# A two-block transformer forward pass in one kernel: the first norm's root moves to VectorE, and the start of the first feed-forward layer is reordered

## What is computed

```python
def rms_norm(x, w):
    xf = x.astype(jnp.float32)
    y = xf * lax.rsqrt(jnp.mean(xf * xf, axis=-1, keepdims=True) + EPS)
    return (y * w.astype(jnp.float32)).astype(x.dtype)

def modulate(x, w, shift, scale):
    return rms_norm(x, w) * (1 + scale[:, None, :]) + shift[:, None, :]

def swiglu(h, w13, w2):
    gu = jnp.einsum('bsd,df->bsf', h, w13)
    g, u = jnp.split(gu, 2, axis=-1)
    return jnp.einsum('bsf,fd->bsd', jax.nn.silu(g) * u, w2)

    c_act = jax.nn.silu(c)
        mod = (jnp.einsum('bd,dn->bn', c_act, w_ada[l]) + b_ada[l]).reshape(b, N_SUB, 3, D_MODEL)
        h = modulate(x, norm_w[l, 0], mod[:, 0, 0], mod[:, 0, 1])
        x = x + 0.5 * mod[:, 0, 2][:, None, :] * swiglu(h, ffn_w13[l, 0], ffn_w2[l, 0])
```

## Time and profile before

| | |
|---|---|
| median of 3 runs | 1054.44 us (1054.14 to 1054.47) |
| profiled execution | 1055.47 us |
| its span, first to last instruction | 1053.6 us |
| PE busy | 1006.0 us, 95% of the span |
| DVE busy | 753.7 us, 72% |
| ACT busy | 534.7 us, 51% |
| POOL busy | 39.3 us, 4% |
| DMA | 215.10 MB, mean 204 GB/s |

### The profile page before, as it was taken

The page is one execution under the profiler, slowest core; times in us unless marked ns, Lnnn a source line. Parts: engine busy times, 40 slices in busy tenths (PEclk is TensorE's granted clock), DMA queues, the critical chain, the costliest instruction groups (busy, mean ns, idle before and its releaser), DMA issues.

```text
span 1053.6 us, 18959 instructions
## 1 busy us (share of the span) xinstructions
PE 1006.0 (95%) x7848; PEld 971.6 (92%) x7848; DVE 753.7 (72%) x1355; ACT 534.7 (51%) x920; POOL 39.3 (4%) x85
## 2 busy tenths in 40 slices
PE   2999999979798999999999999999999999999996
PEld 1999999979797999999999988799899999999996
DVE  4978998857887687685876488546568865575675
ACT  3644654426366555454565445654446554355443
POOL 2000000034400000000000000000000000000000
PEclk9999999989899999999999999999999999999999
DMA  8877899854383455768764545346554555555411
GB/s 329 320 283 298 314 350 354 295 186 161 134 290 136 156 186 180 269 211 194 261 242 160 173 148 200 123 168 171 139 166 160 206 171 189 185 180 208 155 74 41
DMA packets 34533, 215.10 MB, mean 204 GB/s; under 512 B 3725, under 2 KB 7693, under 8 KB 9614
## 3 DMA queue, kind: packets, MB, share of 16 engines
q1 hardware_dynamic: 34446, 213.88, 58.4%
HBM read 211.25 MB, written 2.62 MB: 203 GB/s over the span
## 4 chain that ended last, share of the span: by engine, by line
PE 81%; DVE 5%; DMA 4%; POOL 4%; ACT 3%; issue 3%; SPq 0%; DVEq 0%; POOLq 0%; ACTq 0%
PE bank L210 79%; DMA sb_raw<-wts 3%; PE bank L213 2%; ACT sb_ring L186 1%; POOL sb_nst L189 1%; DVE sb_tq L189 1%; DMA R<-scratch 1%; ACT sb_tmp L186 1%; DVE sb_ring L189 1%; DMA R<-rows 1%; DVE sb_junk L198 1%; POOL sb_st_a L189 0%; POOL sb_st_v L192 0%; POOL sb_nst L192 0%; DVE R L189 0%
## 5 line engine op out<-in xcount | busy, mean ns | idle before, releaser
L210 PE MATMUL bank<-sb_h,sb_ring 128*128 128x256 f32 (+2 forms) x4224 | 523.3, 284 | 10.3 <-DVE sb_tq L189 7.5
L210 PEld LDWEIGHTS bank<-sb_h,sb_ring 128*128 128x128 f32 (+1 forms) x4224 | 513.2, 190 | 14.1 <-DVE sb_tq L189 7.9
L189 DVE TENSOR_TENSOR sb_ring<-sb_raw,sb_ring 128x1024 fp32r<-128x1024 f32 x322 | 385.2, 1212 | 4.0 <-ACT sb_ring L186 3.8
L186 ACT ACTIVATE sb_ring<-sb_raw 128x1024 fp32r<-128x1024 f32 x322 | 320.0, 1043 | 104.6 <-PE bank L210 61.7
L210 PE MATMUL bank<-R_512r,sb_ring 128*128 128x256 f32 x1920 | 234.7, 283 | 0.0
L210 PEld LDWEIGHTS bank<-R_512r,sb_ring 128*128 128x128 f32 x1920 | 231.0, 189 | 0.8 <-issue 0.7
L189 DVE TENSOR_TENSOR sb_tq<-bank,sb_rbc 128x256 f32<-128x256 f32 x107 | 43.1, 421 | 105.3 <-PE bank L210 52.4
L198 DVE CUSTOM_DVE_ANT_0 sb_junk<-sb_raw,sb_csil,sb_cols 128x1024 bf16<-128x1024 f32 x72 | 92.3, 1282 | 1.8
L210 PE MATMUL bank<-R_1024r,sb_ring 128*128 128x256 f32 x768 | 91.5, 281 | 0.0
L210 PEld LDWEIGHTS bank<-R_1024r,sb_ring 128*128 128x128 f32 x768 | 91.3, 188 | 0.0
L210 PE MATMUL bank<-sb_ring,sb_h 128*128 128x512 f32 (+1 forms) x384 | 89.8, 387 | 0.0
(11 more groups left out here) (152 smaller groups left out, 564.4 us busy)
## 6 DMA issues: line engine op xcount, KB each, us to landing
sb_raw<-wts SPq DMA_DIRECT2D x194, 1024.0 KB, 5.0
R<-scratch SPq DMA_DIRECT2D x4, 768.0 KB, 7.8
scratch<-R SPq DMA_DIRECT2D x1, 1536.0 KB
sb_x<-xt SPq DMA_DIRECT2D x2, 512.0 KB, 5.8
out<-R SPq DMA_DIRECT2D x2, 512.0 KB, 2.9
sb_raw<-wts SPq DMA_DIRECT2D x1, 768.0 KB, 4.2
sb_raw<-wts SPq DMA_DIRECT2D x1, 640.0 KB, 3.8
sb_raw<-wts SPq DMA_DIRECT2D x1, 512.0 KB, 3.7
```

What stands on the lines that cost most here:

```text
L186: return Issued(self.e and self.e.activation(o, i, func, **kw))
L189: return Issued(self.e and self.e.tensor_tensor(*a))
L210: return Issued(self.e and self.e.matmul(o, w, m, start=start, stop=stop, skip_group_check=True))
```

## The change

Four things are changed. First, the first norm is made with `x_norm("f1")` in place of `x_norm("f1", True)`: the reciprocal root and both diagonals are issued by VectorE, right behind the variance, and not by GpSimd. VectorE's form of `rsqrt` has one operation for the start value and three rounds of two products and one scalar_tensor_tensor, 10 operations; GpSimd's has 13. Second, the unit of the modulation pair (1, 9) is taken behind the steps of k = 0, no longer ahead of `norm_rows`. Third, `SILU_AT` puts the two halves of Silu(c) ahead of square 0 and square 3, where they stood ahead of square 4 and square 7. Fourth, `xr` is multiplied by the factors and by the column `acol` in one scalar_tensor_tensor; `h_hi` then reads it once, adds the shift column and writes the high part, in one ACT operation where there were two; `h_lo` adds the shift column itself, and is a scalar_tensor_tensor too.

```diff
@@
-SILU_AT = (4, 7)
+SILU_AT = (0, 3)
@@
         self.take_unit()
         self.flush()
-        norm = self.x_norm("f1", True)
-        for _ in range(2):
-            self.take_unit()
-            self.flush()
+        norm = self.x_norm("f1")
+        self.take_unit()
+        self.flush()
         self.norm_rows(norm)
         bk = [b.take() for b in B]
         for k in range(8):
-            if k > 1:
+            if k:
                 self.take_unit()
                 self.flush()
-            if k:
                 self.take_unit()
             self.add("acol", 0, (k,))
             self.add("xr", k)
@@ def h_hi(self, k):
-        xr = m.reg(44 + k, 256)
         e.wait_ge(*self.at("xr", k))
-        e.wait_ge(*self.at("acol", 0, k))
         e.wait_ge(*self.at("ada", k))
-        e.activation(xr, xr, FN.Identity, scale=m.acol[:, k:k + 1], bias=m.mod[:, k:k + 1]).then_inc(
-            *self.up("scalar_own"))
-        e.wait_ge(*self.last())
-        e.activation(m.hk(k)[0], xr).then_inc(*self.up("h_hi", ("h_hi", k)))
+        e.activation(m.hk(k)[0], m.reg(44 + k, 256), FN.Identity, bias=m.mod[:, k:k + 1]).then_inc(
+            *self.up("h_hi", ("h_hi", k)))
@@ def xr(self, k):
-        e.tensor_tensor(m.reg(44 + k, 256), m.x[:, k, :], m.rbc, ALU.mult).then_inc(*self.up("xr", ("xr", k)))
+        e.wait_ge(*self.at("acol", 0, k))
+        e.scalar_tensor_tensor(m.reg(44 + k, 256), m.x[:, k, :], m.acol[:, k:k + 1], m.rbc, ALU.mult,
+                               ALU.mult).then_inc(*self.up("xr", ("xr", k)))
@@ def h_lo(self, k):
-        e.tensor_tensor(lo, m.reg(44 + k, 256), hi.bitcast(F32), ALU.subtract).then_inc(
-            *self.up("h_lo", ("h", "f1", k)))
+        e.scalar_tensor_tensor(lo, m.reg(44 + k, 256), m.mod[:, k:k + 1], hi.bitcast(F32), ALU.add,
+                               ALU.subtract).then_inc(*self.up("h_lo", ("h", "f1", k)))
```

## The result

The changed kernel takes 1048.38 us (median of 4 runs, 1047.96 to 1049.18) against 1054.45 us before, 6.07 us less. The ratio is 0.9937, with a 95% interval of 0.9925 to 0.9949. In a later series on one chip it was 1048.65 against 1055.48 (0.9935, 0.9923 to 0.9948). The forecast was 1048.9.

The account below looks back on a forecast made before the run. PE, busy 95% of the span, was taken as the bound, its long run held back by the start chain. An earlier start (-5.3) and the clock (-0.2) gave -5.5 us: 1048.9 us, range 1047.5 to 1050.9, chance 0.71.

Parts of the forecast that it names:

- What bounds the start: Start of the kernel: a dependent chain delays PE's unbroken run to 26.05 us; starting it earlier moves everything behind.
- The rival by which the gain is not passed on: A later wait, on a load or VectorE between 70 and 200 us, ends at its old time: 1053 to 1054.4; chance 0.04.
- Root and diagonals, pair, `h`: First norm and k = 0: PE starts 5.3 us earlier, 5.0 from root and order, about 0.3 from `h_hi`.
- The form of `h`: Steps of k = 0: one ACT operation of 0.42 us less, two longer VectorE operations; about 0.3 us gained.
- Silu(c) at nothing: ACT at the start: 1.28 us removed, hidden by unit 0 landing at 11.44 and the modulation pair; 0 gained.
- VectorE keeps up: Loop over k: a VectorE round of 5.90 us, `h` of k = 7 ready at 62.0, lead over PE shrinking to 1.3 us.
- no wait is added: Loop over k: PE never waits for VectorE unless a round is over 6.1 us.
- The loads at nothing: Weight units 5 to 7, issued later at first, fall into idle DMA time and hold the pace; 0 lost.
- a sign that was named as one of being wrong: Loop over k: ACT waiting for a unit just ahead of `lo` would show the prediction wrong.
- The clock: PE's slow stretch at the start might shorten, giving back 0.7 us; a third was taken, -0.2.
- its first rival: The clock rises later at the start and at 232 us, losing 1.7 us: about 1050.7; chance 0.14.
- Sum: Whole kernel: -5.3 - 0.2 = -5.5 us, from 1054.44 to 1048.9 us, 0.52% faster.

Follow-up runs that it names:

- second_norm: The changed kernel with root and diagonals of the first mixer's norm also moved from GpSimd to VectorE; 1043.27 us.
- extra_after: The changed kernel with one additional VectorE operation, its result unused, behind `h_lo` of k = 1 to 7; 1050.33 us.
- after_again: The changed kernel run once more, unchanged, in a later series; 1048.65 us, ratio 0.9935 to the kernel before.
- without_silu: The changed kernel with Silu(c) back ahead of squares 4 and 7, and the second table load; 1049.27 us.

## Why the prediction was right, step by step

*What bounds the start.* Right. PE's first product sets the time of all that follows: from the first `silu` to PE's return at the mixer's norm it is 162.81 us before, 162.85 in the changed kernel, and 162.8 to 163.0 in all the others but `second_norm`, which changes that stretch. The rival by which the gain is not passed on is excluded.

*Root and diagonals, pair, `h`.* Right: 14.59 - 9.39 = 5.20 us from the pair to PE's start, where the prediction's rows gave 5.3. The form of `h` gave 0.17 of it, not 0.3.

*Silu(c) at nothing.* This term was mis-sized. The cover that was named, the landing of unit 0 at 11.44, was read from the chain of the earlier trace rows. But in the same profile the sum of squares ended at the same moment, and it was the later one in the four others with the old order. Unit 0 landed at 10.13 to 11.01 us in the thirteen other profiles, earlier than that one profile said, and the term measured about 0.5 us.

*VectorE keeps up.* The round was 5.91 (5.90 forecast), and `h` of k = 7 was ready at 61.81 (62.0). PE was the part that was off. The time from `h` of k = 7 to `silu` is 1.07 us in `extra_after`, where PE waited, and in no profile is it shorter; it was 6.26 before and is 1.12 in the changed kernel. The lead was thus 5.2 us and is 0.05 in the profiled execution (0.00 in `after_again`), not 1.3: a slow stretch of 3.5 us in place of 5.5 brings PE to k = 7 as VectorE finishes. That accounts for about 0.85 of the missing 1.25 us. Where the slow stretch was long, in `without_silu`, 1.2 us of lead were left. So "no wait is added" holds only just.

*The loads at nothing.* Right, although a sign that was named as one of being wrong did appear. In the profiled changed kernel ScalarE waits six times for a weight unit within the loop over k, 3.2 us at the longest, where the kernel before has 1.8. But at every k the high part is done at least 1.0 us before VectorE starts the `lo` that reads it, and VectorE shows no idle time in the loop.

*The clock.* The direction was a guess (-0.2), and a lucky one in the profile, where it gave back 0.9; no median shows it. Over the 12 profiles without a filled start the slow stretch was 3.1 to 6.0 us, with no relation to the part changed; the two slow stretches behind 220 us vary too. This is a good part of the scatter of the single times: of 24 executions of the kernel before in the first series, the 7 with a mean granted clock under 0.990 have a median of 1055.67 us, the other 17 one of 1054.59. The three executions within 0.33 us, which the prediction held against its first rival, were luck: the 24 reach from 1053.27 to 1057.31. In `after_again`, PE's windows at the mixer's norm show a pace of 1.2 GHz until about 231.6, against 228.7 in the first profile of the same program, though PE came back from the same idle time (6.60 and 6.59 us) at the same place:

```profile
226.00:228.00 2.00, 2.00 (x12) 0.50 0.13 53
228.00:230.00 2.00, 2.00 (x11) 0.50 0.00 0
230.00:232.00 2.00, 2.00 (x13) 0.60 0.00 0
```

And in the first profile of the changed kernel:

```profile
226.00:228.00 2.00, 2.00 (x10) 0.50 0.33 139
228.00:230.00 2.00, 2.00 (x16) 0.83 0.00 0
230.00:232.00 2.00, 2.00 (x19) 1.00 0.00 0
```

Same program, same idle time before, 3.2 us more at the slow pace (225.45 to 231.6, against 225.78 to 228.7), and the profiled execution took 1049.78 in place of 1047.99 us. The rule of the Trainium skill in "TensorE: Matmul & The Clock Gate", section "What's actually happening", that the monitor runs freely and does not start with the kernel, fits this: the trace agrees in that one program spent 6.1 and 2.9 us at the norm (at the start 3.3 and 3.5). No run here tests that cause against another.

*Sum.* 5.2 + 0.5 = 5.7 us are shown by parts. The medians give 6.1 and 6.8, with intervals of about 1.3 us on each side; the rest, 0.4 and 1.1 us, is within them, and was not told apart. The forecast of 5.5 us came as 5.3 of that and a guess of 0.2; the 0.5 us of Silu(c) stand where the guess was, so the closeness of the number is in part luck.

## What to carry to other kernels

A chain of tiny dependent operations belongs on the engine that can run it at 0.20 us a step, ahead of that engine's long operations, if the matrix engine is waiting for it; here the first such chain was worth 2.5 us by itself and 5.0 with the modulation pair moved behind it, the second 5.4 us, with the fall of the clock that it took away. Look for long operations that stand between the chain's last input and its first use, and move behind that use whatever is needed only a round later. Before more is taken from the start, compare when each engine is ready at the end of the loop: here VectorE's lead went from 5.2 us to nothing, and a further gain that brings forward only PE's side, like a shorter slow stretch, is worth nothing unless VectorE's round gets shorter. A gain that moves VectorE's own row as well is still passed on: in `after_again` the pair starts 0.41 us earlier than in the first profile of the same kernel, and `h` of k = 7 is ready 0.40 us earlier.

## What the runs showed of the hardware that was not expected

The same program spent 2.9 us in one execution and 6.1 us in another at the slow pace after the same idle time, and products that fill most of the idle time ahead of the first run of products left a slow stretch of 1.8 us in one profile and of 4.2 in another. The first load lands between 10.13 and 11.44 us in the 14 profiles, so that one profile cannot say which of two things that end within 0.5 us is the later. An additional operation on VectorE in each round of the kernel before went with a median 1.9 us lower, of which 1.3 are left when executions with the same mean granted clock are compared, unexplained.
